# Attention in a hybrid encoder layer: the products with the values in two groups per tile instead of eight

## The reference, cut to what matters

```python
# A: 8 local heads, window of 128 to each side, sink logit, relative bias
s = einsum('bqhgd,bkhd->bhgqk', qb, kb) * scale + bias     # 128 queries x 384 keys
m = maximum(max(s), sink); e = exp(s - m)
p = e / (sum(e) + exp(sink - m))
oa = einsum('bhgqk,bkhd->bqhgd', p, vb)
# B: 8 full heads, normalised and rotated q and k
s = einsum('bqhgd,bkhd->bhgqk', qb, k) * scale             # 128 queries x all keys
ob = einsum('bhgqk,bkhd->bqhgd', softmax(s), v)
x += concat(RMSNorm_A(oa), RMSNorm_B(ob)) @ W_out          # then experts, embeddings, final norm
```

## Time and profile before

| | before |
|---|---|
| median of three executions | 1595.22 us |
| the profiled execution | 1595.72 us |
| its span | 1593.9 us |
| TensorE busy, matmuls | 1445.4 us (91%) |
| VectorE busy | 932.5 us (59%) |
| ScalarE busy | 722.8 us (45%) |
| sample attention | about 280 to 553 us of the span |
| prompt attention | about 560 to 663 us of the span |

### The profile page before, as it was taken

The page is one execution under the profiler, slowest core; times in us unless marked ns, Lnnn a source line. Parts: engine busy times, 40 slices in busy tenths (PEclk is TensorE's granted clock), DMA queues, the critical chain, the costliest instruction groups (busy, mean ns, idle before and its releaser), DMA issues. The chain is left out here.

```text
span 1593.9 us, 21545 instructions
## 1 busy us (share of the span) xinstructions
PE 1445.4 (91%) x7320; PEld 1017.7 (64%) x7320; DVE 932.5 (59%) x1324; ACT 722.8 (45%) x1157; POOL 182.1 (11%) x255
## 2 busy tenths in 40 slices
PE   5899997999999789599998689999999999939997
PEld 4778885655565455378887556666666666627885
DVE  5454443777777577523356756766776676643544
ACT  4244433667676567422223444544544544423332
POOL 1111111000000000100001211121121121021110
PEclk9999998899999979899998889999999999968999
DMA  7533353511113143254433847788788788752331
GB/s 259 97 112 112 112 181 129 189 65 65 64 66 107 56 163 117 79 200 158 136 115 119 271 146 250 254 270 267 251 267 269 254 260 270 240 164 100 132 133 66
DMA packets 118847, 261.53 MB, mean 164 GB/s; under 512 B 7648, under 2 KB 37472, under 8 KB 115720
## 3 DMA queue, kind: packets, MB, share of 16 engines
q1 hardware_dynamic: 110592, 233.55, 41.8%
q0 software_dynamic: 7168, 25.17, 6.8%
q10 hardware_dynamic: 1032, 2.10, 1.2%
HBM read 194.20 MB, written 66.58 MB: 164 GB/s over the span
## 5 line engine op out<-in xcount | busy, mean ns | idle before, releaser
L1798 DVE TENSOR_TENSOR moe_w_lo<-ring,moe_w_hi 128x2048 fp32r<-128x2048 f32 x96 | 220.3, 2296 | 163.1 <-ACT moe_w_hi L1737 163.1
L1737 ACT ACTIVATE moe_w_hi<-ring 128x2048 fp32r<-128x2048 f32 x96 | 183.7, 1914 | 205.1 <-PE moe_p_g L1920 86.4
L1469 PE MATMUL mix_p_big<-kept_out_w,mix_m_hi 128*128 128x512 f32 x384 | 126.6, 411 | 4.6 <-DVE mix_m_lo L1344 2.4
L529 PE MATMUL proj_p_out<-proj_w_hi,proj_h_hi 128*128 128x512 f32 x264 | 110.4, 418 | 8.4 <-DVE proj_qn L428 8.4
L1928 PE MATMUL moe_p_gu<-ring,moe_xT_r 128*64 128x512 f32 x512 | 116.9, 598 | 0.0
L529 PE MATMUL proj_p_out<-proj_w_lo,proj_h_hi 128*128 128x512 f32 x264 | 105.6, 400 | 0.0
L529 PE MATMUL proj_p_out<-proj_w_hi,proj_h_lo 128*128 128x512 f32 x264 | 105.1, 398 | 0.0
L1018 DVE TENSOR_REDUCE sample_ntop<-sample_p_s 128x1 f32<-128x1024 f32 x64 | 78.2, 1222 | 38.9 <-PE sample_p_s L840 38.1
L854 PEld LDWEIGHTS sample_p_t<-sample_ident_r,sample_probs_r 128*128 128x128 f32 x688 | 73.0, 141 | 23.4 <-ACT sample_probs L956 6.7
L1469 PEld LDWEIGHTS mix_p_big<-kept_out_w,mix_m_hi 128*128 128x128 f32 x384 | 73.2, 196 | 21.4 <-DVE mix_m_lo L1344 2.6
L854 PE MATMUL sample_p_t<-sample_ident_r,sample_probs_r 128*128 128x128 f32 x688 | 80.2, 246 | 5.0 <-ACT sample_probs L956 2.6
(11 more groups left out here) (318 smaller groups left out, 3131.2 us busy)
## 6 DMA issues: line engine op xcount, KB each, us to landing
ring<-in_w_gate SPq DMA_DIRECT2D x32, 1024.0 KB, 5.6
ring<-in_w_up SPq DMA_DIRECT2D x32, 1024.0 KB, 7.6
ring<-in_w_down SPq DMA_DIRECT2D x32, 1024.0 KB, 6.3
qT_d<-proj_qT SPq DMA_DIRECT2D x12, 1024.0 KB, 3.9
proj_x<-in_x SPq DMA_DIRECT2D x12, 512.0 KB, 4.2
proj_w_raw<-in_w_in SPq DMA_DIRECT2D x8, 768.0 KB, 6.6
kT_d<-proj_kT SPq DMA_DIRECT2D x12, 512.0 KB, 3.6
ahead_q<-qT_d SPq DMA_DIRECT2D x6, 1024.0 KB, 5.0
```

The source lines that it names most:

```text
L529: last = pe.matmul(p_out[:, cols], h[:, s, k, :], w[:, k, cols], start=(k == 0 and n == 0), stop=(k == KC - 1 and n == 2))
L1469: mm = pe.matmul(p_out[:, cols], m[:, s, k, :], ww[:, k, cols], start=(k == 0 and n == 0), stop=(k == KC - 1 and n == 2))
L1737: act.activation(w_hi[:, at % SPLIT], raw[:, at % RAW], ACT.Copy).then_inc(hi_made, 1)
L1798: dve.tensor_tensor(w_lo[:, at % SPLIT], raw[:, at % RAW], w_hi[:, at % SPLIT].bitcast(F32), ALU.subtract).then_inc(lo_made, 1)
```

## The change

The full heads' products of a tile move from steps 3 to 7 of the next tile into one group at step 5. The local heads' products move from steps 11, 12 and 13 into one group at step 12. The waits ahead of them move along. Nothing is added to or taken from the arithmetic, and no other engine's stream changes.

```diff
+            B_AT, A_AT = [5], HEADS + 4
+
             def values_b(i, j):
-                if j == 3:
+                part, size = B_AT.index(j), n // len(B_AT)
+                if part == 0:
                     for b in range(2):
                         pe.wait_ge(t_out[b], half(i + 1))
                     pe.wait_ge(oT_out[A], i + 1)
-                share_of = [0] + [round(n * k / 5) for k in range(1, 6)]
-                values(None, B, list(range(share_of[j - 3], share_of[j - 2])), 0, n)
+                values(None, B, list(range(part * size, (part + 1) * size)), 0, n)
...
-                    if 3 <= j < HEADS and not first:
+                    if j in B_AT and not first:
                         values_b(i - 1, j)
                     if j == HEADS + 2 and not first:
                         turn_o_b(i - 1)
-                    if HEADS + 3 <= j < HEADS + 6:
+                    if j == A_AT:
                         lo, hi = edges(first, last)
-                        if j == HEADS + 3:
-                            for b in range(2):
-                                pe.wait_ge(t_out[b], half(i) + HEADS // 2)
-                            if not first:
-                                pe.wait_ge(oT_out[B], i)
-                        b = j - HEADS - 3
-                        if lo <= b < hi:
-                            values(s, A, [b], lo, hi)
+                        for b in range(2):
+                            pe.wait_ge(t_out[b], half(i) + HEADS // 2)
+                        if not first:
+                            pe.wait_ge(oT_out[B], i)
+                        values(s, A, list(range(lo, hi)), lo, hi)
```

More of the change, by code:

```diff
@@ L917, in _ @@
                 turn(n - 1, head, False, False, True)
-            for j in range(3, HEADS):
+            for j in B_AT:
                 values_b(n - 1, j)
```

## The result

The changed kernel takes 1608.15 us (median of four, 1606.36 to 1610.71) against 1595.73 before in the same comparison: the ratio is 1.0086, 95% interval 1.0067 to 1.0105, so slower by 0.67 to 1.05%. The prediction had 1599.0 and a range to 1604.5. The profiled execution took 1606.36 us, its span is 1604.6 us against 1593.9.

The account below looks back on a forecast made before the run. TensorE was taken as the bound in steps with values products, the chain through VectorE and ScalarE elsewhere. Sample +1.75 and prompt +2.05 gave +3.8 us on 1595.7; less 0.5 for the median, 1599.0, range 1586 to 1604.5.

Parts of the forecast that it names:

- The walk through the local heads: Inner sample tile: TensorE followed start by start, new waits for exponentials before the group, head 8's scores at 423.6; chance 0.50.
- The fixed cost that grouping gives back: TensorE: going into and out of a group costs 0.26 us, so four fewer full-head groups save 1.04 us per inner sample tile.
- The rival by which TensorE stays the bound: Whole kernel: TensorE stays the bound and fixed costs come back, -7 to -14 us, 1581 to 1588; chance 0.21.
- the last rival: Starved engines cost 0.4 to 0.6 us more per tile, or TensorE's clock falls in the prompt: 1604 to 1608; chance 0.10.
- a loss that can be told: Whole kernel: slower by more than about 0.2% or 3.2 us, what a measurement can tell from no change; chance 0.45.
- Local heads, +0.25 us a tile: Inner sample tile: 1.04 us given back is spent on about 1.1 us of new waiting and 0.2 at VectorE.
- Full heads, nothing: Inner sample tile, heads 10 to 15: sum 11.99 us against 11.95 before; the 0.44 us given back is eaten.
- Prompt, +2.05 us: Prompt stage: 0.85 us in the third tile, 0.4 each in the second and fourth, full heads 0.1 us a tile.

Follow-up runs that it names:

- one transpose: Kernel before, with one transpose of the identity put between the two blocks of each group of two: 1608.57 us, a single execution.
- three groups: Kernel before, with full heads' products in three groups at steps 3, 5, 7: ratio 0.9995; the same in the sample only: 1589.98 us, 0.9969.
- Filling the waits and the ends: Changed kernel plus useless identity transposes in TensorE's waits at steps 3 and 4 and at the stages' ends: 1601.54 us, against 1606.52 for the changed kernel.
- this part alone: Kernel before, with only the full heads' products grouped at step 5, the local heads' left at steps 11, 12, 13: 1603.7 us, ratio 1.0055.
- the kernel with this part alone: Kernel before, with only the local heads' products grouped at step 12, the full heads' left at steps 3 to 7: 1597.29 us, ratio 1.0014.
- the one with 3.65: Kernel before, with full heads' products in two equal groups at steps 3 and 6, local heads' spread as before: 1599.1 us, ratio 1.0026.
- the second trace: Changed kernel run again unaltered, beside the kernel with waits and ends filled: 1606.52 us, ratio 1.0072 to before.

## Why the prediction was wrong in size

**The direction and the mechanism were right.** The walk through the local heads holds almost to the row: the new wait of 0.70 us (0.8 forecast), the group at 7.93 us after the tile's start (forecast 415.22-407.34 = 7.88), head 8's scores at 16.41 (16.26). The fixed cost that grouping gives back is real (0.26 forecast; measured 0.55 for two groups, and 0.37 with one transpose, itself included). The rival by which TensorE stays the bound, the tiling rule's, is refuted for one group of 32; with three groups TensorE does stay the bound, and the gain in the sample's tiles is there.

**The step that failed is the sum, which had no term for the granted clock.** It stood only as a clause in the last rival, at a chance of 0.10 with its companion, and for the prompt alone. Filling the waits and the ends is worth 5.0 us of the 11.1 us by which the changed kernel's median lay over before's; the 6.2 us that are left compare with the forecast's 3.8. In the six sample tiles of the first trace the clock's falls are 3.1 of 6.5 us. That the direction came out right is partly luck: the walk's gains and losses nearly cancel, and the forecast itself gave a loss that can be told only 0.45.

**Local heads, +0.25 us a tile.** Measured 0.45 with this part alone. The walk was right to head 8's scores within 0.15 us. The mis-sized term is VectorE behind the burst: the two maxima were taken 0.7 us apart and start 0.88 apart (424.17 and 425.05). The 0.7 is from a row where a copy follows the maximum, not a second maximum; why the second one starts later is not shown. Together with head 6's scores, which are 0.08 us later than in the walk, VectorE comes to head 8 0.50 us late, not 0.22.

**Full heads, nothing.** 0.09 us a tile in the kernel with this part alone, right within what the rows allow. That is for the six tiles; at the ends of the stages, where the clock fell, the same kernel lost more.

**Prompt, +2.05 us.** In the profiled execution the prompt took 106.95 us from its first scores to its last transposes against 101.08, +5.9. Its third tile, the one that was walked, lost 24.53-23.32 = 1.2 us against 0.95. The fourth and the end lost 3.8 us against 0.5. There the lower clock and the starving come together. With the local heads' group alone, whose forecast here was 0.1 us, the fourth tile with its end lost 3.8 us too, at the same granted clock of 0.85; its group of 8 matmuls takes 3.59 us, where a group of 8 at full clock takes 1.94. With the full heads' group alone it lost 1.9 us. Each is one trace, and the clock is below 1.00 there before the change as well (0.94), so how much comes from the change is not shown. With the ends filled the prompt still took 4.7 us more than before, so part of it stays open.

**The sum of the profile.** From the first scores of the sample to the last transposes of the prompt the changed kernel needs 14.1 us more (674.14-277.68 against 661.74-279.42). The first sample tile has -0.3 of them, the second to seventh 6.5, the eighth with the end of the sample 2.1 and the prompt 5.9. The 14.1 us are more than the 10.7 by which the span grew; the rest of the program, which is the same, was 3.4 us shorter in that execution.

## What to carry to other kernels

When three engines pass work along two slots deep, the long engine's spare work is also what fills its waits: collecting it into one piece gives back the cost of switching but takes the filler away and leaves the others idle for the length of the piece. Group only up to the time that the slots ahead cover (here the layout with groups up to 2.8 us held and the one with 3.65 did not), and check each stage by itself, since what paid in the sample did not in the prompt. New waits on TensorE can have a second price besides their length, so look at the granted clock beside the waits, and test it by filling them.

## What the runs showed of the hardware

TensorE's granted clock fell to its lower level in the middle of a stage without any gap longer than 0.70 us in that tile: in the third tile of the changed kernel the 8.17 us from its first scores to the group were busy for 6.68, and in the fifth, where no fall came, 6.39 of 7.93. In the second trace the third tile had it again, and the seventh and eighth. In the eighth tile with the full heads' group alone the scores at 519.31 are slow (0.58 us for a row that lasts 0.38 at full clock), and the longest wait in that tile until then is 0.39 us, so the new wait is not needed for a fall. With the 1.1 us of waits filled by transposes, no sample tile had one in two traces, and with the ends filled too the kernel was 5.0 us faster for work of no use.

A single transpose of 128 columns between matmuls that use 64 columns of the array costs 0.37 us, several times its place in a row of its own kind (about 0.08). The Trainium skill's rule that changing the tiling mode drains TensorE (TensorEngine Tiling (Array Packing), Key Properties) fits this; it gives no figure, and no run here shows that the change of mode is the reason.
